# Score, index, bias and first attention products placed behind a quarter of a unit of other matmuls; the bias table's load ahead of the key unit

## What is computed

```python
# sparse attention (per block of 128 queries)
rel = relu(einsum('bqhd,bsd->bqhs', q_idx, k_idx))           # index products, 16 heads of 64
score = einsum('bqh,bqhs->bqs', w_idx, rel) * INDEXER_SCALE
score = where(causal, score, NEG_INF)
_, sel = top_k(score, 64)
logits = einsum('bqhd,bqkhd->bhqk', q, k[sel]) * HEAD_DIM ** -0.5
logits += rel_bias[t5_bucket(dist)]                          # the bias table
p = softmax(logits); out = einsum('bhqk,bqkhd->bqhd', p, v[sel])
...
# experts
qh = (x @ wq).reshape(128, 8, 2, 128)                        # query units
s1 = einsum('thd,kd->thk', qh[:, :, 0], sub_keys[0])         # score products
s2 = einsum('thd,kd->thk', qh[:, :, 1], sub_keys[1])
v1, i1 = top_k(s1, 16); v2, i2 = top_k(s2, 16)               # key search
best, pos = top_k(v1[..., :, None] + v2[..., None, :], 16)
out = sum(softmax(best) * gelu(x . u[expert]) * v[expert])
```

## Time and profile before

| | us |
|---|---|
| median of 3 runs | 2902.71 |
| lowest and highest run | 2898.66, 2905.43 |
| span of the profiled execution, first to last instruction | 2895.8 |

### The profile page before, as it was taken

One profiled execution on the slowest core, in us unless ns is written; L12 is line 12 of the kernel. 1 busy time (PEld: TensorE's weight loads), 2 busy tenths in 40 slices (PEclk: granted clock), 3 DMA queues, 4 the chain that ended last, 5 costly groups with the idle time before them and its releaser, 6 DMA issues.

```text
span 2895.8 us, 46048 instructions
## 1 busy us (share of the span) xinstructions
PE 2784.9 (96%) x19224; PEld 2627.5 (91%) x19224; DVE 1940.6 (67%) x2900; ACT 1363.5 (47%) x2223; POOL 388.4 (13%) x360
## 2 busy tenths in 40 slices
PE   7999999999999999999989999999999999999996
PEld 6999989888999998999989999998888999988785
DVE  7556578554435545564658657767887888878886
ACT  5356454455545334444453124434555555555554
POOL 0000010211110000005000002221222111113320
PEclk9999999999999999999999999999999999999998
DMA  5444455433325554544534569998999988899894
GB/s 225 172 155 153 159 158 193 135 109 101 100 97 185 180 177 162 188 146 162 180 118 161 186 233 360 365 356 332 368 374 374 341 326 322 319 356 366 339 355 145
DMA packets 109678, 668.44 MB, mean 231 GB/s; under 512 B 25776, under 2 KB 26312, under 8 KB 31552
## 3 DMA queue, kind: packets, MB, share of 16 engines
q1 hardware_dynamic: 83808, 496.08, 46.8%
q0 software_dynamic: 24512, 164.97, 15.6%
q10 hardware_dynamic: 1152, 4.47, 0.4%
HBM read 651.54 MB, written 13.30 MB: 230 GB/s over the span
## 4 chain that ended last, share of the span: by engine, by line
PE 71%; DVE 13%; DMA 9%; ACT 5%; issue 2%; SPq 0%; POOL 0%; DVEq 0%; ACTq 0%
PE PS L1093 71%; DVE WL L1723 5%; DMA raw<-in_pv 4%; DVE m L1714 4%; DMA m<-in_pv,keep 3%; ACT WH L2497 2%; ACT m L2478 1%; DVE m L1967 1%; PE PS L1096 1%; DMA m<-s_kk 1%; ACT m L2479 1%; DVE m L1964 0%; DMA raw<-in_w_kv 0%; DVE m L2318 0%; ACT L2478 0%
## 5 line engine op out<-in xcount | busy, mean ns | idle before, releaser
L1723 DVE TENSOR_TENSOR WL<-raw,WH 128x1024 fp32r<-128x1024 f32 x804 | 988.1, 1237 | 591.2 <-ACT WH L2497 589.2
L2497 ACT CAST WH<-raw 128x1024 fp32r<-128x1024 f32 x804 | 836.9, 1046 | 529.2 <-PE PS L1093 357.3
L1093 PE MATMUL PS<-m_4096r,WH 128*128 128x256 f32 x5184 | 976.9, 289 | 24.5 <-DVE WL L1723 12.9
L1093 PEld LDWEIGHTS PS<-m_4096r,WH 128*128 128x128 f32 x5184 | 812.8, 193 | 44.4 <-issue 24.9
L1093 PE MATMUL PS<-m_4096r,WL 128*128 128x256 f32 x2592 | 736.2, 284 | 0.0
L1093 PE MATMUL PS<-m_8192r,WH 128*128 128x256 f32 (+1 forms) x2560 | 559.8, 313 | 8.8 <-issue 5.4
L1093 PE MATMUL PS<-WH,m_896r 128*128 128x512 f32 x1536 | 521.8, 392 | 12.7 <-DVE m_896r L2411 9.1
L1093 PEld LDWEIGHTS PS<-m_4096r,WL 128*128 128x128 f32 x2592 | 499.2, 193 | 0.0
L1093 PEld LDWEIGHTS PS<-m_8192r,WH 128*128 128x128 f32 x2560 | 398.3, 194 | 10.7 <-issue 6.0
L1093 PE MATMUL PS<-m_8192r,WL 128*128 128x192 f32 (+1 forms) x1792 | 404.6, 272 | 0.0
L1093 PE MATMUL PS<-WL,m_896r 128*128 128x512 f32 x1024 | 400.3, 391 | 0.0
(11 more groups left out here) (246 smaller groups left out, 1807.6 us busy)
## 6 DMA issues: line engine op xcount, KB each, us to landing
raw<-in_pu SPq DMA_DIRECT2D x128, 1024.0 KB
raw<-in_pv SPq DMA_DIRECT2D x128, 1024.0 KB
raw<-in_w_qkv SPq DMA_DIRECT2D x48, 1024.0 KB
raw<-in_w_o SPq DMA_DIRECT2D x48, 1024.0 KB
raw<-in_w SPq DMA_DIRECT2D x40, 1024.0 KB
raw<-in_w_z SPq DMA_DIRECT2D x32, 1024.0 KB
raw<-in_w_kv SPq DMA_DIRECT2D x16, 1024.0 KB
raw<-in_w_q SPq DMA_DIRECT2D x16, 1024.0 KB
```

The lines of the kernel that those rows point to most:

```text
L1093: return e.matmul(o, l, x, start=start, stop=stop)
L1723: tt(WL[:, k, :], raw[:, n % NRAW, h * 1024:h * 1024 + 1024], WH[:, k, :].bitcast(F), ALU.subtract).then_inc(S["lo"], 1)
L2497: e.copy(WH[:, k, :], raw[:, n % NRAW, h * 1024:h * 1024 + 1024]).then_inc(S["hi"], 1)
```

## The change

In `run`, the step `bias` is split: `bias_load` (GpSimd's two loads) stays ahead of the key unit, the rest goes behind the first quarter of index unit 0. `ki_out` is split too: the copies stay, the transposes and the index weights (`ki_turn`) go behind its second quarter. The index products of unit i go behind the first and second quarter of unit i + 1, those of the last unit into the first `KQ` unit. `attend` begins with a `yield` and is chained to the attention weights, so the first `av` stands behind the first quarter of pool unit 0, and each later one a quarter later than before. `qs_out` is split into `qe_out`, ScalarE's first copy, which stays behind the unit, and `qs_out`, products and second copy, behind the first quarter of the next unit (the last behind the first eighth of the first expert unit).

```diff
     def attend(self):
+        yield
         for h in range(8):
...
+    def scored(self, i, st):
+        self.do("qs_out", i)
+        st["s"] += 1
...
             for _ in self.unit(PEER + 128 * half + j, per=6, later=later if half == 0 and j >= 62 else None):
+                if st["s"] < 16:
+                    self.scored(15, st)
...
-        do("bias")
+        do("bias_load")
         drain(self.units(KIWI, 1, "ki_out"))
-        for i in range(8):
-            drain(self.unit(QI_ + i))
-            do("qi_out", i)
-            for hh in (2 * i, 2 * i + 1):
-                for p in range(2):
-                    do("index", hh, p)
+        for i in range(9):
+            for part, _ in enumerate(self.unit(QI_ + i)):
+                if part < 2 and i:
+                    for p in range(2):
+                        do("index", 2 * i - 2 + part, p)
+                elif part < 2:
+                    do(("bias", "ki_turn")[part])
+            if i < 8:
+                do("qi_out", i)
+            else:
+                do("kq_out", 0)
         for i in range(16):
-            drain(self.unit(KQ + i))
-            do("kq_out", i)
+            if i:
+                drain(self.unit(KQ + i))
+                do("kq_out", i)
             do("topk", 2 * i)
             do("topk", 2 * i + 1)
-        together(self.weights(), self.values2())
-        do("pool_loads")
-        pool = self.units(PU, 8, "pu_out")
-        together(self.attend(), pool)
+        together(chain(self.weights(), self.attend()), chain(self.values2(), self.pooled()))
...
-        for i in range(16):
-            if i >= 2:
-                for n, _ in enumerate(self.unit(WQ + i)):
-                    if i < 5 and n % 2 == 0:
-                        next(ho, None)
-                    if i >= 5 and n < 3:
-                        next(st["keys"])
+        do("qe_out", 0)
+        do("qe_out", 1)
+        for i in range(2, 16):
+            for n, _ in enumerate(self.unit(WQ + i)):
+                if n == 0:
+                    for k in (0, 1) if i == 2 else (i - 1,):
+                        self.scored(k, st)
+                if i < 5 and n % 2 == 0:
+                    next(ho, None)
+                if i >= 5 and n < 3:
+                    next(st["keys"])
             if i == 4:
                 drain(ho)
-            do("qs_out", i)
-            st["s"] += 1
+            do("qe_out", i)
```

More of the change, by code:

```diff
@@ L417, in values2, with pooled @@
                 self.do("v2_turn", i - 1)
+    def pooled(self):
+        self.do("pool_loads")
+        yield from self.units(PU, 8, "pu_out")
     def weights(self):
@@ L664 @@
                  ("stat", 1)),
-    "small_dve": (("sg_min", 1), ("sg_g", 1), ("sg_gc", 2), ("keep", 1), ("bias_v", 1), ("ki", 1), ("ki_copy", 1), ("wi", 1),
+    "small_dve": (("sg_min", 1), ("sg_g", 1), ("sg_gc", 2), ("keep", 1), ("ki", 1), ("ki_copy", 1), ("bias_v", 1), ("wi", 1),
                   ("mask", 2), ("ln1_var", 1), ("ln1_rs", 1)),
@@ L1500, in bias, with ki_turn @@
                 mm(PS[0:8, 2, 0:384], RB, HOT, True, True).then_inc(S["bias_mm"], 1)
-            def ki_out(_):
+            def ki_turn():
                 p.wait_ge(*at("ki", 1))
@@ L1702, in tensor_program @@
                   "iv_product": iv_product, "dn_in": dn_in, "dn_uc": dn_uc, "dn_w": dn_w, "dn_u": dn_u_, "dn_o": dn_o,
-                  "dn_yss": dn_yss, "dn_ybc": dn_ybc, "bias": bias, "ki_out": ki_out, "index": index,
+                  "dn_yss": dn_yss, "dn_ybc": dn_ybc, "bias": bias, "ki_turn": ki_turn, "index": index,
                   "v2_turn": v2_turn, "aw": aw, "at": at_, "av": av, "pm": pm, "mean": mean, "stat": stat_,
@@ L2463, in vector_program @@
                   "iv_step": iv_step, "iv_out": iv_out, "dn_decay": dn_decay, "dn_uc": dn_uc, "dn_low": dn_low, "dn_o": dn_o, "dn_yss": dn_yss, "dn_yn": dn_yn, "y_split": y_split, "x1_out": x1_out,
-                  "bias": bias, "ki_out": ki_out, "index": index, "topk": topk, "v2_turn": v2_turn, "aw": aw, "an": an,
+                  "bias": bias, "ki_out": ki_out, "ki_turn": ki_turn, "index": index, "topk": topk, "v2_turn": v2_turn, "aw": aw, "an": an,
                   "at": at_, "av": av, "pm": pm, "r1_out": r1_out, "mean_add": mean_add, "mean_out": mean_out, "dev": dev, "stat": stat_, "ln1": ln1, "h2": h2,
@@ L2744, in h_out, with qe_out @@
                 e.copy(STG[:, t, c * 512:c * 512 + 512], PS[:, 4 + it % 4, :]).then_inc(S["h_out"], 1)
-            def qs_out(i):
+            def qe_out(i):
                 a.wait_ge(*at("used", done(WQ + i)))
@@ L2751, in qs_out @@
                 e.copy(f(76 + i % 4, 256), PS[:, i % 2, 0:256]).then_inc(S["qe"], 1)
+            def qs_out(i):
                 a.wait_ge(*at("qs", i + 1))
@@ L2863, in scalar_program @@
                   "v2_out": v2_out, "aw": aw, "av": av, "pu_out": pu_out, "pm": pm, "dev": dev, "ln1": ln1, "h2": h2,
-                  "h_out": h_out, "qs_out": qs_out, "s_exp": s_exp, "u_sum": u_sum, "u_out": u_out, "g_hots": g_hots, "g_apply": g_apply,
+                  "h_out": h_out, "qe_out": qe_out, "qs_out": qs_out, "s_exp": s_exp, "u_sum": u_sum, "u_out": u_out, "g_hots": g_hots, "g_apply": g_apply,
                   "sp_gate": sp_gate, "c_split": c_split, "v_evac": v_evac, "end": end}).run()
@@ L2981, in x_load, with bias_load @@
                 e.dma_start(X1, D["xT"]).then_inc(S["ld_res"], 16)
-            def bias():
+            def bias_load():
                 g_.wait_ge(*at("y_lo", 9))
@@ L2987, in bias @@
                 e.dma_start(RB, D["rb"]).then_inc(S["ld_hot"], 16)
+            def bias():
                 g_.wait_ge(*at("bias_v", 1))
@@ L3090, in gpsimd_program @@
             Plan({"hn_square": hn_square, "qk_out": qk_out, "iv_turn": iv_turn, "iv_store": iv_store,
-                  "iv_scale": iv_scale, "iv_out": iv_out, "dn_low": dn_low, "dn_y": dn_y, "gate": gate, "x_load": x_load, "bias": bias, "ki_out": ki_out,
+                  "iv_scale": iv_scale, "iv_out": iv_out, "dn_low": dn_low, "dn_y": dn_y, "gate": gate, "x_load": x_load, "bias_load": bias_load, "bias": bias, "ki_out": ki_out,
                   "pool_loads": pool_loads, "pu_out": pu_out, "sub_load": sub_load, "h_store": h_store,
```

## The result

| | before | after |
|---|---|---|
| median of 5 runs beside each other, us | 2902.71 | 2892.13 |
| lowest and highest, us | 2898.66, 2905.43 | 2891.29, 2897.99 |
| span of the profiled execution, us | 2895.8 | 2896.2 |

The ratio is 0.9969, with a 95% interval of 0.9957 to 0.998: 0.31% or 9.0 us faster, where the prediction said 17.4. (The ratio goes by all five runs of each; the two medians alone lie 10.6 us apart.) The forecast 2885.3 us lies 6.8 us too low. The time lies inside the range, but near its upper end, and nearly half of the gain is missing.

What follows compares the result with a forecast made beforehand. TensorE, 71% of the chain, was taken to bound the kernel. Terms 1.2 - 0.1 + 4.2 + 1.0 + 2.4 + 1.2 + 1.3 + 6.8 - 0.6 = 17.4 us took span 2895.8 to 2878.4, median 2885.3 us; range 2881 to 2893.

Steps and rivals of the forecast that it cites:

- the index products: Index units: eight waits of 0.62 us go, eight more turns of 0.10 us come; +4.2 us (2.3 to 5.0).
- (1): Query units: VectorE has no usable lead, units 5 to 15 stay near 6.98 us; 10.8 us won, 2891.9 us; chance 0.12.
- (2): Behind query units 0 and 1: the slow clock stays; 15.9 us won, 2886.8 us; chance 0.26.
- the pause that stood ahead of the transposes: Key unit to index unit 0: the wait for VectorE's copy stays, moved transposes cost one more turn; -0.1 us.
- The bias product: Key unit: 1.92 us of the 3.5 us go, the product returns at 0.74 us inside the next unit; +1.2 us.
- The first attention product: Before pool unit 0: a quarter of that unit fills TensorE's wait for VectorE's copy of the last values; +1.0 us.
- the unit pair: Query units 0 and 1: one pause instead of two, slow clock behind it taken to go; +2.4 us, 0.9 if it stays.
- The first copy can't be earlier: Query units 0 and 1: ScalarE's first copy cannot move forward, so TensorE's 1.64 us pause stays.
- VectorE catches TensorE: Last query units: VectorE at 6.98 us a unit uses up its lead at the very end; -0.6 us (0 to -2).
- I keep that distance: Whole run: the median stays 6.9 us above the profiled span, so 2878.4 becomes 2885.3 us.
- (3): All moved places: the waits only change place; about 5 us won, 2898 us; chance 0.06.
- (4): All 41 insertions: each costs far more than a 0.1 us turn; 9.3 us slower, 2912.0 us; chance 0.06 with the unseen.

Runs made afterwards that it cites:

- behind: The changed kernel with the index products back behind their own unit, all else moved; 2886.91 us, ratio 0.9957 to before.
- four: The changed kernel with all four index products of a unit together behind the next unit's first quarter; 2879.14 us, ratio 0.9935 to before.
- best: Changed kernel plus index products together, two key-search rounds in query units 11 to 15, query copies 0 and 1 ahead of ScalarE's casts; 2884.46 us, ratio 0.9934.
- query: The kernel before with only the query units' part of the change; 2892.77 us, ratio 0.9965 to before.
- again: The changed kernel run once more without an edit; 2889.28 us, ratio 0.9956 to before.

## Why the prediction was right or wrong

**The term that failed: the index products.** The step was "one insertion of four becomes two of two", priced at 8 x 0.10 us. It let the 0.86 us of four products be divided without a loss and charged only the second turn. What it left out stands in the code: a product reads partitions from `64 * (hh % 2)` on, and the change cuts by head, so each group is left with one half. Measured with four together: 7.33 - 6.81 = 0.52 us a unit gained. Measured with two and two of one half: 0.50 us lost. Over eight units the term is -4.0 instead of +4.2; that is 8.2 us, and 8.4 are missing by the ratio. Its stated bounds, 2.3 to 5.0, were worked out from turns and weight loads alone, so they missed it as well. The Trainium skill (TensorE: Matmul & The Clock Gate, section Part 3: Packing small matmuls) says that matmuls which use part of the rows can run at once in the same array. The traces here agree: 0.87 us for four products of two halves, 1.51 for four of one half.

That the time still lies inside the range is luck. The range reached up to 2893 us to take in rivals (1) and (2), and neither of them happened.

**The other terms.** The stretch from the last cast of x to the experts also loses the 0.6 us of score product 15, which moves behind it. So the forecast's 17.4 mean 18.0 there. Without the index term it is 13.8, and `behind` has 14.0; with it as forecast 18.0, and `four` has 18.1; with it as measured 9.8, and the change has 10.0. In detail: the key unit starts behind a wait that the prediction took as 1.6 us. From start to start it is 1.57; the row counts from the modelled end of the matmul before:

```profile
1083.64 0.51 PE L1110 MATMUL PS<-m_4096r,WH 128*128 128x256 f32 x2 [1.42 <-DVE m_4096r L2064]
```

Index unit 0 does carry the pause that stood ahead of the transposes. The profile puts it to "issue", but the unit's first matmul starts 0.11 us behind the end of VectorE's copy of the key unit (1089.70 + 0.42 us), much as the transposes did before (0.06 us). The transposes come back at their price. The bias product does not: with the way in and out (0.09 us ahead of it, 0.10 in the first pair behind) it takes 0.92 us, where 0.74 were taken. So 0.9 us are won up to the first index copy instead of 1.1:

```profile
1090.23 0.47 PE L1110 MATMUL PS<-m_4096r,WH 128*128 128x256 f32 x2 [0.56 <-issue]
...
1091.83 0.81 PE L1110 MATMUL PS<-m,m 32*8 32x384 f32 x2
1092.56 0.51 PE L1110 MATMUL PS<-m_4096r,WH 128*128 128x256 f32 x2
...
1094.10 0.38 PE L1113 MATMUL PS<-cons,m 128*128 128x128 f32 x2
1094.24 0.48 PE L1110 MATMUL PS<-m_4096r,WH 128*128 128x256 f32 x2
```

The first attention product stands behind a quarter of pool unit 0, and nothing waits between (against the earlier trace rows):

```profile
1308.90 0.88 PE L1113 MATMUL PS<-cons,m 128*128 128x128 f32 x6 [1.35 <-DVE m L1734]
1309.53 0.48 PE L1110 MATMUL PS<-m_4096r,WH 128*128 128x256 f32 x2
...
1311.04 0.83 PE L1110 MATMUL PS<-m,m 128*128 128x128 f32 x6
```

From the first key copy to the first query copy it is 333.5 us against 334.5: +1.0 as forecast. Behind the unit pair (against the earlier trace rows) the 1.64 us stay. The profile puts them down to a subtraction now, but ScalarE's copy of unit 0 ends at 1493.89, just ahead of the start, and `best` shows that this copy is the cause. "The first copy can't be earlier" holds only for the order that the change leaves on ScalarE. TensorE's timeline:

```profile
1493.94 0.51 PE L1110 MATMUL PS<-m_8192r,WH 128*128 128x256 f32 x2 [1.64 <-DVE WL L1740]
...
1495.48 1.06 PE L1110 MATMUL PS<-m 128*128 128x128 f32 x8
```

The clock stays at 1.00, as two stretches there show (length, busy times, granted clock, DMA share, GB/s):

```profile
1494.00:1496.00 2.00, 2.00 (x17) 2.00 (x18) 1.92 (x2) 1.11 (x2) 0.00 (x0) 1.00 0.47 98
1496.00:1500.00 4.00, 4.00 (x36) 4.00 (x36) 0.79 (x2) 2.25 (x4) 0.00 (x0) 1.00 1.01 416
```

Units 6 to 13 follow each other at 6.20 us (6.31 forecast: two score products come to 0.44 us, the way around included). Since they are faster, VectorE catches TensorE one unit earlier, and the last two copies come at 6.98 us, VectorE's own pace. The list of TensorE's waits in the query units has the pair's pause and these two, 1.1 us together:

```profile
PE PS L1110 <- DVE WL L1740: 2.7, 3, 1.6
```

From the first query copy to the first expert matmul the stage went from 104.9 to 92.8 us; 0.6 of the 12.0 are the last score products, 11.4 are won, and 11.1 were forecast. A part of the 11.4 may be luck: 1.1 of them were the slow clock in the one trace of before.

**The step from the span to the median.** "I keep that distance", 6.9 us, happened to do no harm, because it was applied to the same execution that the sum was made against. But it is 1.8 us that lie around every span and 5.1 us of one short execution. Runs of a kernel scattered more than the 3 us that the prediction allowed: later runs of before went from 2895.1 to 2912.6 us.

**The rivals.** (1) VectorE without a lead: false; its lead lasted up to unit 13, as the working had it within one unit. (2) The clock drop stays: false in all ten traces that keep the 1.64 us; but whether before always had that drop is not known, for `query` shows that a drop is not bound to the code. (3) Waits that only change place: true at index unit 0 and behind the unit pair, both as forecast, and nowhere else. (4) Insertions that cost far more than a turn: false as a rule, and true for one kind. Transposes, attention and score products came in at their price and the bias product 0.2 us above it; 16 of the 41 insertions, the index ones, cost 0.51 us each more than forecast. That is above the 0.42 us from which it decides, but only on 16 and by another mechanism than weights loaded again. The prediction's test "index units at 6.8 us, no wait on the copies" told it at once: the waits had gone and the units had grown.

## What to carry to other kernels

Before you split a group of small matmuls, ask what runs beside what in it: products of 64 partitions in different halves share the array, and a group cut so that each part keeps one half costs twice. A group's price may be divided only along a line that leaves its pairs whole; here one group of four behind a quarter (`four`) gains 0.65 to 0.67%, where the change gains 0.31 to 0.44%. And when a stretch of the trace repeats within 0.1 us while whole runs scatter by 10, make the account in that stretch.

## What was not expected of the hardware

- float32 products of 64 partitions and 128 or 256 columns: four in both halves 0.86 to 0.87 us, four in one half 1.51, two in one half 0.85, two side by side 0.42 (128 columns) and 0.63 (256 columns). In a group of four the halves kept their own order: the third product in the list started 0.014 us behind the first (`four`).
- Going out of a running stream of 256-column matmuls to such a group and back costs 0.18 to 0.19 us, for two products or four, and 0.19 to the one bias product of 32 partitions; to 128-row products and transposes 0.08 to 0.1.
- A pause of 2.5 us of TensorE was followed by the 1.2 GHz level in one trace (`query`, granted clock 0.50, 1.4 us lost) and not in another (before, 2.59 us). The pause of 2.7 us ahead of the first expert query unit stands in all thirteen traces; in ten the granted clock fell to 0.50 at most 0.7 us before or 1.5 us after its end, and in the change's first trace, `query` and `best` it stayed at 1.00. From the first key copy to the first query copy that cost nothing (333.5 us in the change's first trace and in `again`). A single pause of 1.42 us (eleven traces) or 1.64 us (ten) was never followed by it; the double one of before, 1.64 and 0.74 us, was.
- The same code of the expert layers took 1295.6 to 1310.3 us, and three traces of one kernel alone spread over 6.6 us.
